# Three chunks instead of two open the later stages of a four-stage float32 block, and VectorE turns two groups of x

## The chip, the cores and the metric

The kernel runs on one core of a Trainium2 chip. The metric is device time in microseconds for one execution, the median of several runs. TensorE multiplies (PE in the profile, PEld its weight loads), VectorE is DVE, ScalarE is ACT, GpSimd is POOL, and the sync engine SP issues the DMAs. SBUF is the on-chip memory; the eight banks of PSUM take TensorE's results.

## What is computed

256 tokens of width 2048 go through two layers of a first block and one layer of a second, all float32. Cut to what matters here:

```python
def first_block(x, ...):
    for layer in range(2):
        h = rms_norm(x, mix_pre_g[layer])
        m = pool_conformer_mixer(h, ...) if layer == 0 else short_conv_mixer(h, ...)
        x = x + rms_norm(m, mix_post_g[layer])
        h = rms_norm(x, ffn_pre_g[layer])
        x = x + rms_norm(sq_relu_mlp(h, ffn_w1[layer], ffn_w2[layer]), ffn_post_g[layer])
    return x

def short_conv_mixer(h, w_in, conv_w, w_out):
    z = h @ w_in                       # b_gate, c_gate, u of 2048 each
    return (b_gate * causal_depthwise_conv(c_gate * u, conv_w)) @ w_out

def sq_relu_mlp(h, w1, w2):
    a = relu(h @ w1)                   # 2048 -> 8192
    return (a * a) @ w2                # 8192 -> 2048

def hybrid_layer(x, ...):              # the second block
    proj = rms_norm(x, norm_g) @ w_in  # q, k, v, z_a, u_b, v_b, z_b, g_a, g_b
    # q and k are normed per head; attention, a gated unit, two projections, and
    return x + merged @ w_out
```

## The kernel before

**Stages.** There are five: the first mixer, the first MLP, the short convolution, the second MLP, and the second block. `STAGE` holds their first chunks: 0, `C_M0`, `C_L1`, `C_M1`, `C_L2`. A chunk is 512 columns of a weight matrix (`chunk_table`), and its result fills two PSUM banks, one for each tile of 128 tokens.

**Steps.** A step is 256 rows of a chunk's weights. Each weight is split in two parts, w_hi (ScalarE, `split_hi`, L800) and w_lo (VectorE, `split_lo`, L818, which needs w_hi), and so is each activation, in buffers A and B. A step takes 12 matmuls of 128x512: two k-tiles, two token tiles, and lo x hi, hi x lo, hi x hi (L839 to L841). A chunk has 8 steps, or 4 where its depth is 1024. `SEQ` is the order of all steps, written by hand; `POS` gives a step's place in it. The text counts steps from the start of a stage. There are 6 slots for split weights and 3 for raw ones; a raw slot holds two steps.

**Order of work.** Every engine's program is a loop over the same steps. In its loop for step s, ScalarE or VectorE first splits the weights of step s + 3 and then does what the tables put at step s. Their queues are strictly in that order: what stands in the loop for step 34 comes after the split of step 37's weights. At a chunk's last step ScalarE waits until TensorE has done the chunk and evicts it (L1101). So the split of the fourth step after a chunk's last step stands behind the eviction, on ScalarE and, since w_lo needs w_hi, on VectorE.

**The opening of a stage.** x is updated in four groups of 512 columns, turned, scaled and split into A before the first matmul of a stage can use a group. Two chunks share the opening: their first four steps each, which need groups 0 and 1, then their last four, which need group 2 (first two of them) and group 3. TensorE turns groups 0 and 1 tile by tile (`turn_tile`, L907) and group 2 with `turn_x` (`turn`, L890) into the four small banks 4 to 7; VectorE turns group 3 in blocks of 32 by 256 (`turn_last`, L1525), four blocks at each of four steps. `hi_turned` and `lo_turned` cast it into A.

**Turning the hidden tiles.** In an MLP stage a pair of up chunks makes two tiles of 512 hidden features; four down chunks use them. ScalarE evicts a tile to z with a relu, GpSimd squares it, and VectorE turns it, 16 blocks in `TURN_STEPS` = 8 steps, two at each (`turn_hidden`, `turn_blocks`, L1944). `TURN_AT` gives the first step. After the last, ScalarE casts the high part (L1456) and VectorE the low part (L1984). In an MLP stage the order is chunks 0 and 1 (up, first pair), 2 and 3 (up, second pair), 4 to 7 (down, first pair). Chunk 3 takes steps 24 to 31 and chunk 4 steps 32 to 35. A down chunk's first two steps need the pair's first tile, its last two the second tile.

**Short convolution and last stage.** Chunks 0 to 2 of the short convolution make c, u and b of the first 512 features; VectorE multiplies c and u, turns the product and b, convolves (`short_conv`), and gates. In the last stage chunks 0 to 3 make q and k: ScalarE evicts and squares, VectorE sums per head (L2047) at the step after the chunk's end, scales (L2060) two steps later, and turns from the step that `QK_TURNS` gives, as (steps after the chunk's end, steps to spread over).

**Banks.** Chunk c uses main banks 2 (c % 2) and the next, and may start when chunk c - 2 has been evicted.

## Time and profile before

| | us |
|---|---|
| median of 3 runs | 2673.4 |
| lowest, highest | 2673.11, 2673.76 |
| the profiled run | 2673.97 |
| span of the profiled execution | 2672.2 |
| TensorE busy | 2665.8 |
| VectorE busy | 1960.7 |
| ScalarE busy | 1289.1 |
| GpSimd busy | 286.3 |

The span is the time from the first to the last instruction on the core; the run is a little longer. Busy times are those of one execution. A matmul's row gives a duration that overlaps the next matmul's, so TensorE's pace is read from the starts of its rows. The idle time in brackets at the end of a row is the engine's own, ahead of that row, with what ended it.

### The profile page before, as it was taken

All of it is one profiled execution on the core that took longest, in us unless ns stands there. A gap on an engine that the chain in (4) does not pass through costs nothing.

```text
span 2672.2 us, 31094 instructions
## 1 busy us (share of the span) xinstructions
PE 2665.8 (100%) x11905; PEld 2207.6 (83%) x11905; DVE 1960.7 (73%) x2706; ACT 1289.1 (48%) x1625; POOL 286.3 (11%) x263
## 2 busy tenths in 40 slices
PE   9999999999999999999999999999999999999999
PEld 7888888888888888888888888888888888888887
DVE  6888867666766787777777676668668869985574
ACT  6875544444444454444544444344455545544452
POOL 4841100000000010000100000000011001000000
PEclk9999999999999999999999999999999999999999
DMA  7555665555655556555556655555555655565554
GB/s 257 189 174 189 209 202 189 189 189 189 205 188 190 199 185 214 190 196 196 190 190 205 204 186 184 198 189 192 190 186 189 208 178 174 175 217 192 189 203 143
DMA packets 268148, 515.57 MB, mean 193 GB/s; under 512 B 8498, under 2 KB 28260, under 8 KB 267492
## 3 DMA queue, kind: packets, MB, share of 16 engines
q1 hardware_dynamic: 267732, 513.34, 57.3%
q8 instruction: 97, 1.59, 0.2%
q14 instruction: 47, 0.39, 0.0%
q10 hardware_dynamic: 272, 0.26, 0.0%
HBM read 511.47 MB, written 2.10 MB: 192 GB/s over the span
## 4 chain that ended last, share of the span: by engine, by line
PE 99%; DVE 0%; DMA 0%; ACT 0%; issue 0%; SPq 0%; DVEq 0%; ACTq 0%
PE bank L839 32%; PE bank L841 32%; PE bank L840 32%; PE bank L890 0%; PE bank L907 0%; PE bank L1062 0%; DMA x_res<-in_x 0%; DMA w_raw<-in_ab_w_in 0%; DVE w_lo L818 0%; PE bank L1076 0%; DVE tap_product L2083 0%; DVE z L2071 0%; PE bank L1048 0%; PE bank L1086 0%; PE bank L1085 0%; PE bank L1027 0%
## 5 line engine op out<-in xcount | busy, mean ns | idle before, releaser
L818 DVE TENSOR_TENSOR w_lo<-w_raw,w_hi 128x1024 fp32r<-128x1024 f32 x950 | 1182.4, 1263 | 439.5 <-ACT w_hi L800 433.0
L800 ACT ACTIVATE w_hi<-w_raw 128x1024 fp32r<-128x1024 f32 x954 | 973.0, 1056 | 615.6 <-PE bank L841 417.9
L839 PE MATMUL bank<-w_hi,A_lo 128*128 128x512 f32 x2432 | 950.6, 391 | 0.9 <-DVE w_lo L808 0.8
L841 PE MATMUL bank<-w_hi,A_hi 128*128 128x512 f32 x2432 | 946.8, 389 | 0.0
L840 PE MATMUL bank<-w_lo,A_hi 128*128 128x512 f32 x2432 | 946.5, 389 | 0.0
L839 PE MATMUL bank<-w_hi,B_lo 128*128 128x512 f32 x1408 | 548.6, 390 | 0.0
L841 PE MATMUL bank<-w_hi,B_hi 128*128 128x512 f32 x1408 | 547.8, 389 | 0.0
L840 PE MATMUL bank<-w_lo,B_hi 128*128 128x512 f32 x1408 | 547.8, 389 | 0.0
L839 PEld LDWEIGHTS bank<-w_hi,A_lo 128*128 128x128 f32 x2432 | 456.6, 188 | 97.7 <-DVE w_lo L808 2.2
L841 PEld LDWEIGHTS bank<-w_hi,A_hi 128*128 128x128 f32 x2432 | 456.5, 188 | 95.2
L840 PEld LDWEIGHTS bank<-w_lo,A_hi 128*128 128x128 f32 x2432 | 456.7, 188 | 93.5
L841 PEld LDWEIGHTS bank<-w_hi,B_hi 128*128 128x128 f32 x1408 | 264.3, 188 | 54.9
L839 PEld LDWEIGHTS bank<-w_hi,B_lo 128*128 128x128 f32 x1408 | 264.3, 188 | 54.7
L840 PEld LDWEIGHTS bank<-w_lo,B_hi 128*128 128x128 f32 x1408 | 264.3, 188 | 54.6
L1944 DVE STREAM_TRANSPOSE conv_out<-z 32x256 f32<-32x256 f32 x512 | 223.2, 436 | 10.5
L1101 ACT ACTIVATE z<-bank,small 128x512 f32<-128x512 f32 x108 | 68.5, 686 | 328.0 <-PE bank L841 320.8
L2247 POOL TENSOR_TENSOR z<-z 128x512 f32<-128x512 f32 x64 | 65.3, 1041 | 1094.1 <-ACT z L1101 1094.1
L1971 DVE TENSOR_TENSOR acc<-bank,acc 128x512 f32<-128x512 f32 x96 | 61.8, 686 | 85.7 <-PE bank L841 85.7
L2128 POOL TENSOR_TENSOR acc<-acc,gain_row 128x512 f32<-128x512 f32 x32 | 41.0, 1298 | 518.3 <-ACT bank L1172 477.7
L1456 ACT ACTIVATE B_hi<-conv_out 128x512 fp32r<-128x512 f32 x64 | 37.1, 628 | 99.6 <-DVE conv_out L1944 99.6
L2122 POOL TENSOR_TENSOR small<-small,neg_half 128x1 f32<-128x1 f32 (+2 forms) x21 | 34.3, 1633 | 298.9 <-DVE small L1498 280.7
L1944 DVE STREAM_TRANSPOSE conv_in<-z 32x256 f32<-32x256 f32 x128 | 55.8, 436 | 2.6
(176 smaller groups left out, 991.6 us busy)
## 6 DMA issues: line engine op xcount, KB each, us to landing
w_raw<-in_ffn_w SPq DMA_DIRECT2D x256, 1024.0 KB, 5.3
w_raw<-in_w_in SPq DMA_DIRECT2D x88, 1024.0 KB, 5.0
w_raw<-in_sc_w_in SPq DMA_DIRECT2D x48, 1024.0 KB, 5.1
w_raw<-in_ab_w_out SPq DMA_DIRECT2D x16, 1024.0 KB, 5.0
w_raw<-in_sc_w_out SPq DMA_DIRECT2D x16, 1024.0 KB, 5.0
w_raw<-in_w_out SPq DMA_DIRECT2D x16, 1024.0 KB, 5.0
w_raw<-in_ab_w_in SPq DMA_DIRECT2D x26, 512.0 KB, 4.9
w_raw<-in_ab_w_in SPq DMA_DIRECT2D x8, 1024.0 KB, 5.1
```

The source lines that it names most:

```text
L800: e.activation(w_hi[:, s % SPLIT_SLOTS, :], raw_step(s), ACT.Copy).then_inc(hi_made, 1)
L818: e.tensor_tensor(w_lo[:, slot, :], raw_step(s), w_hi[:, slot, :].bitcast(F32), ALU.subtract).then_inc(lo_made, 1)
L839: e.matmul(ps, lo[:, kt, tok], wh, start=first, stop=False)
L840: e.matmul(ps, hi[:, kt, tok], wl, start=False, stop=False)
L841: ins = e.matmul(ps, hi[:, kt, tok], wh, start=False, stop=last)
L1101: e.activation(out(tt), main_bank(c, tt), func, scale=rs(layer_of(c))[:, tt:tt + 1]).then_inc(act_took(c, tt), 1)
L1456: e.activation(halves["B"][0][:, kt:kt + 2, :], h_T[:, 2 * h:2 * h + 2, :], ACT.Copy).then_inc(hi_cast("h", layer, b, j, h), 1)
L1944: ins = e.transpose(dst[feat, :, :].rearrange("p k (t c) -> p t k c", t=NT)[:, :, :, tok], src[tok, :, :].rearrange("p t (k c) -> p t k c" ...
L1971: e.tensor_tensor(out, main_bank(c, tt), out, ALU.add).then_inc(dve_took(c, tt), 1)
L2122: e.tensor_tensor(out, cols(n, "mean", *key), neg_half[:, 0:n], ALU.pow).then_inc(root_made(*key), 1)
L2128: e.tensor_tensor(out, out, gain_row[:, c], ALU.mult).then_inc(gained(p, n, tt), 1)
L2247: e.tensor_tensor(z[:, s, tt, :], z[:, s, tt, :], z[:, s, tt, :], ALU.mult).then_inc(squared(layer, b, j, tt), 1)
```

## The change

The opening of stages 1 to 4 takes three chunks: the first four steps of chunks 0, 1 and 2, then the last four of chunks 0 and 1 in turns of two steps, then the last four of chunk 2. Chunk 0 ends with step 17 (it was 11), chunk 1 with step 19 (15), chunk 2 with step 23 as before. Chunk 2 uses the small banks 4 and 5, and starts when the last cast from them is done. TensorE turns groups 0 and 1 of x only. VectorE turns group 2 at steps 3 to 7 and group 3 at steps 8 to 12 (`X_TURNS`), and the casts stand at steps 9 and 14 (`X_HALVES`).

What hangs on the ends of chunks 0 and 1 moves: the hidden tiles of an MLP's first pair are turned in 7 steps each, at steps 19 to 25 and 27 to 33 (they were turned at 13 to 20 and 22 to 29), and cast at steps 26 and 34 (21 and 30). In the short convolution the product is turned at steps 20 to 27 (16 to 23) and b at 28 to 35 (24 to 31). In the last stage the four tiles of q and k are turned at steps 21 to 25, 26 to 30, 31 to 35 and 36 to 40 (15 to 20, 21 to 26, 27 to 31 and 35 to 39).

```diff
 TURN_STEPS = 8
+BY_VECTOR = (2, 3)
+X_TURNS = {2: (3, 5), 3: (8, 5)}
+X_HALVES = {2: 9, 3: 14}
 STEP_K = 2
...
-QK_TURNS = [(3, 6), (5, 6), (3, 5), (3, 5)]
+QK_TURNS = [(3, 5), (6, 5), (7, 5), (4, 5)]
...
-                for half in range(2):
-                    SEQ += [(c, 4 * half + i) for c in (first, first + 1) for i in range(4)]
-                rest = first + 2
+                SEQ += [(first + n, i) for n in range(3) for i in range(4)]
+                for half in range(2, 4):
+                    SEQ += [(c, 2 * half + i) for c in (first, first + 1) for i in range(2)]
+                SEQ += [(first + 2, i) for i in range(4, 8)]
+                rest = first + 3
...
+        def hidden_steps(b):
+            return 7 if b == 0 else TURN_STEPS
+
         TURN_AT = {}
         for layer in range(2):
             free = 0
             for b in range(NB):
                 for j in range(2):
                     TURN_AT[layer, b, j] = max(free, S_END[up_chunk(layer, b, j)] + 1)
-                    free = TURN_AT[layer, b, j] + TURN_STEPS + 1
+                    free = TURN_AT[layer, b, j] + hidden_steps(b) + 1
...
-        x_T = conv_out_flat[:, GK * TOK:2 * GK * TOK].rearrange("p (k t) -> p k t", k=GK)
+        x_T = {2: conv_out_flat[:, GK * TOK:2 * GK * TOK].rearrange("p (k t) -> p k t", k=GK),
+               3: conv_out_flat[:, 0:GK * TOK].rearrange("p (k t) -> p k t", k=GK)}
...
+        THIRD = [STAGE[p] + 2 for p in range(1, 5)]
+
         def main_bank(c, tt):
-            return bank[2 * (c % 2) + tt]
+            return bank[4 + tt if c in THIRD else 2 * (c % 2) + tt]
...
-            if i == 0 and c >= 2:
-                for tt in which:
-                    sem, value = taken(c - 2, tt)
-                    e.wait_ge(sem, value)
+            if i == 0 and c in THIRD:
+                e.wait_ge(lo_cast.sem, lo_cast.of("pre", THIRD.index(c) + 1, 1, 1, 1))
+            elif i == 0 and c >= 2:
+                for before in (c - 4, c - 2) if c - 2 in THIRD else (c - 2,):
+                    for tt in which:
+                        sem, value = taken(before, tt)
+                        e.wait_ge(sem, value)
...
-                if (c, i) == (C_L1 + 1, 0):
-                    turn_x(2, 2)
...
-                if (c, i) == (STAGE[p] + 1, 0):
-                    hi_x(p, 2)
-                if (c, i) == (STAGE[p] + 1, 1):
+                n = POS[c, i] - S0[STAGE[p]]
+                if n == 5:
                     statistics(p)
-                if (c, i) == (STAGE[p], 4):
-                    hi_turned(p)
+                for g in BY_VECTOR:
+                    if n == X_HALVES[g]:
+                        hi_turned(p, g)
...
-            def turn_last(p, n):
-
-                if n == 0:
-                    e.wait_ge(x_made.sem, x_made.of(p - 1, NG - 1, 1))
-                tok = slice(32 * n, 32 * n + 32)
-                for q in range(4):
-                    feat = slice(32 * q, 32 * q + 32)
-                    ins = e.transpose(x_T[feat, :, :].rearrange("p k (t c) -> p t k c", t=NT)[:, :, :, tok],
-                                      x[tok, :, D - CH:].rearrange("p t (k c) -> p t k c", k=GK)[:, :, :, feat])
-                if n == 3:
-                    ins.then_inc(x_turned(p), 1)
-
-            def lo_turned(p):
+            def lo_turned(p, g):
...
-                n = POS[c, i] - S0[STAGE[p]] - 3
-                if 0 <= n < 4:
-                    turn_last(p, n)
-                if (c, i) == (STAGE[p] + 1, 3):
-                    lo_turned(p)
+                at_step = POS[c, i] - S0[STAGE[p]]
+                for g in BY_VECTOR:
+                    if at_step == X_HALVES[g]:
+                        lo_turned(p, g)
+                for g in BY_VECTOR:
+                    first, steps = X_TURNS[g]
+                    n = at_step - first
+                    if 0 <= n < steps:
+                        if n == 0:
+                            e.wait_ge(x_made.sem, x_made.of(p - 1, g, 1))
+                        ins = turn_blocks(e, x[:, :, g * CH:(g + 1) * CH], x_T[g], n, steps)
+                        if n == steps - 1:
+                            ins.then_inc(x_turned(p, g), 1)
...
-                if part == 2 and j < NG:
-                    if i == 0:
-                        e.wait_ge(dve_took.sem, dve_took.of(c - 1, 1))
-                        if j > 0:
-                            e.wait_ge(short_made.sem, short_made.of(j - 1, SHORT_K - 1, GK - 1))
-                    ins = turn_blocks(e, z[:, z_slot("c", j), :, :], short_in[:, :, SPAD:], i)
-                    if i == TURN_STEPS - 1:
-                        ins.then_inc(c_turned(j), 1)
+                for j in range(NG):
+                    made = C_L1 + 3 * j + 1
+                    n = POS[c, i] - S_END[made]
+                    if 0 <= n < TURN_STEPS:
+                        if n == 0:
+                            e.wait_ge(dve_took.sem, dve_took.of(made, 1))
+                            if j > 0:
+                                e.wait_ge(short_made.sem, short_made.of(j - 1, SHORT_K - 1, GK - 1))
+                        ins = turn_blocks(e, z[:, z_slot("c", j), :, :], short_in[:, :, SPAD:], n)
+                        if n == TURN_STEPS - 1:
+                            ins.then_inc(c_turned(j), 1)
                 for k in range(NG):
-                    n = POS[c, i] - S0[C_L1 + 3 * k + 3] - (1 if k == NG - 1 else 0)
+                    n = POS[c, i] - S0[C_L1 + 3 * k + 3] - (4 if k == 0 else 1 if k == NG - 1 else 0)
...
-            ins = turn_blocks(e, z[:, z_slot("h", layer, b, j), :, :], h_T, n)
-            if n == TURN_STEPS - 1:
+            ins = turn_blocks(e, z[:, z_slot("h", layer, b, j), :, :], h_T, n, hidden_steps(b))
+            if n == hidden_steps(b) - 1:
                 ins.then_inc(turned(layer, b, j), 1)
...
                 for b in range(NB):
                     for j in two:
                         n = POS[c, i] - TURN_AT[layer, b, j]
-                        if 0 <= n < TURN_STEPS:
+                        if 0 <= n < hidden_steps(b):
                             turn_hidden(e, layer, b, j, n)
-                        if n == TURN_STEPS:
+                        if n == hidden_steps(b):
...
```

The first place is VectorE's queue in an MLP stage, around the end of chunk 3 (z is the tile that is turned, B_lo the low part of the hidden tile). Before, from the split of step 34 on:

```order
L818 TENSOR_TENSOR w_lo<-w_raw,w_hi 128x1024 [waits hi_made]
L1944 STREAM_TRANSPOSE conv_out<-z 32x2x4x32 [waits lo_cast,squared]
L1944 STREAM_TRANSPOSE conv_out<-z 32x2x4x32
L818 TENSOR_TENSOR w_lo<-w_raw,w_hi 128x1024 [waits hi_made]
L1944 STREAM_TRANSPOSE conv_out<-z 32x2x4x32 x2
```

Now, from the split of step 35 to what follows the split of step 37:

```order
L829 TENSOR_TENSOR w_lo<-w_raw,w_hi 128x1024 [waits hi_made]
L1944 STREAM_TRANSPOSE conv_out<-z 32x2x4x32 x2
L829 TENSOR_TENSOR w_lo<-w_raw,w_hi 128x1024 [waits hi_made]
L1944 STREAM_TRANSPOSE conv_out<-z 32x2x4x32 x3
L829 TENSOR_TENSOR w_lo<-w_raw,w_hi 128x1024 [waits hi_made]
L1984 TENSOR_TENSOR B_lo<-conv_out,B_hi 128x512 [waits hi_cast] x2
```

Before, the second hidden tile had been cast four steps earlier and the first tile of the next pair was being turned here; now the last pieces of the second tile, with one of three blocks, and its cast stand behind the splits of steps 35 to 37.

The second place is ScalarE's queue at the same steps, from the eviction of chunk 3 (bank2, bank3) on. Before:

```order
L1101 ACTIVATE z<-bank2,small 128x512 [waits step_done,turned,root_made]
L1101 ACTIVATE z<-bank3,small 128x512 [waits step_done]
L800 ACTIVATE w_hi<-w_raw 128x1024 [waits step_done]
L800 ACTIVATE w_hi<-w_raw 128x1024 [waits step_done,raw_loaded1]
L800 ACTIVATE w_hi<-w_raw 128x1024 [waits step_done]
L800 ACTIVATE w_hi<-w_raw 128x1024 [waits step_done,raw_loaded2]
L1179 ACTIVATE acc<-bank0 128x512 [waits step_done]
```

Now:

```order
L1104 ACTIVATE z<-bank2,small 128x512 [waits step_done,turned,root_made]
L1104 ACTIVATE z<-bank3,small 128x512 [waits step_done]
L811 ACTIVATE w_hi<-w_raw 128x1024 [waits step_done]
L811 ACTIVATE w_hi<-w_raw 128x1024 [waits step_done,raw_loaded1]
L811 ACTIVATE w_hi<-w_raw 128x1024 [waits step_done]
L1459 ACTIVATE B_hi<-conv_out 128x512 [waits turned]
L1459 ACTIVATE B_hi<-conv_out 128x512
```

The high part of the second hidden tile has moved behind the eviction and the three splits after it.

The third place is VectorE's queue in the last stage, behind the split of step 23 (acc<-z are the blocks of q and k, the reductions are the sums per head, z<-z the scaling). Now:

```order
L2060 TENSOR_TENSOR z<-z,small 128x512 [waits root_made]
L2060 TENSOR_TENSOR z<-z,small 128x512
L2047 TENSOR_REDUCE small<-conv_in 128x8 [waits square_made]
L1501 TENSOR_SCALAR small<-small 128x8 [waits total_made]
L829 TENSOR_TENSOR w_lo<-w_raw,w_hi 128x1024 [waits hi_made]
L1944 STREAM_TRANSPOSE acc<-z 32x2x4x32 [waits normed]
L1944 STREAM_TRANSPOSE acc<-z 32x2x4x32 x2
L829 TENSOR_TENSOR w_lo<-w_raw,w_hi 128x1024 [waits hi_made]
L2060 TENSOR_TENSOR z<-z,small 128x512 [waits root_made]
```

Before, that work of the first chunk stood from step 12 on:

```order
L2047 TENSOR_REDUCE small<-conv_in 128x8 [waits square_made]
L1498 TENSOR_SCALAR small<-small 128x8 [waits total_made]
L818 TENSOR_TENSOR w_lo<-w_raw,w_hi 128x1024 [waits hi_made] x2
L2060 TENSOR_TENSOR z<-z,small 128x512 [waits root_made]
L2060 TENSOR_TENSOR z<-z,small 128x512
L818 TENSOR_TENSOR w_lo<-w_raw,w_hi 128x1024 [waits hi_made]
L1944 STREAM_TRANSPOSE acc<-z 32x2x4x32 [waits normed]
```

The scaling of the first tile and the sums of the second now stand between the same two splits, and the first blocks are turned at step 21 instead of 15.

## Rows read from the trace of the kernel before

**Rows 1.** The page: busy time and count, granted clock in 40 slices, chain.

```profile
PE 2665.8 (100%) x11905; PEld 2207.6 (83%) x11905; DVE 1960.7 (73%) x2706; ACT 1289.1 (48%) x1625; POOL 286.3 (11%) x263
...
PEclk9999999999999999999999999999999999999999
...
PE 99%; DVE 0%; DMA 0%; ACT 0%; issue 0%; SPq 0%; DVEq 0%; ACTq 0%
```

**Rows 2.** TensorE's waits: line, waited for: us in total, times, longest.

```profile
PE bank L942 <- POOL neg_half L2147: 1.6, 1, 1.6
```

**Rows 3.** Timeline of TensorE, first MLP: start, duration, engine, line, operation, count.

```profile
261.69 0.39 PE L841 MATMUL bank<-w_hi,A_hi 128*128 128x512 f32 x1
261.92 1.03 PE L890 MATMUL bank<-ident,x_res 128*128 128x128 f32 x8
...
266.01 0.39 PE L841 MATMUL bank<-w_hi,A_hi 128*128 128x512 f32 x1
...
271.00 0.39 PE L839 MATMUL bank<-w_hi,A_lo 128*128 128x512 f32 x1
...
303.63 0.39 PE L839 MATMUL bank<-w_hi,A_lo 128*128 128x512 f32 x1
```

**Rows 4.** Timeline of VectorE in the opening of the first MLP.

```profile
260.24 1.78 DVE L1525 STREAM_TRANSPOSE conv_out<-x_res 32x256 f32<-32x256 f32 x4
...
275.08 1.66 DVE L1537 SCALAR_TENSOR_TENSOR A_lo<-conv_out,par,A_hi 128x256 fp32r<-128x256 f32 x4
```

**Rows 5.** Timeline of the last stage from its step 16 on.

```profile
2043.37 0.39 PE L839 MATMUL bank<-w_hi,A_lo 128*128 128x512 f32 x1
...
2047.06 1.22 DVE L818 TENSOR_TENSOR w_lo<-w_raw,w_hi 128x1024 fp32r<-128x1024 f32 x1 [2.44 <-ACT w_hi L800]
...
2048.20 1.21 DVE L2047 TENSOR_REDUCE small<-conv_in 128x8 f32<-128x1024 f32 x1
...
2049.64 1.33 DVE L1944 STREAM_TRANSPOSE acc<-z 32x256 f32<-32x256 f32 x3
...
2050.99 1.23 DVE L818 TENSOR_TENSOR w_lo<-w_raw,w_hi 128x1024 fp32r<-128x1024 f32 x1
...
2052.25 1.34 DVE L1944 STREAM_TRANSPOSE acc<-z 32x256 f32<-32x256 f32 x3
...
2054.74 1.28 DVE L2060 TENSOR_TENSOR z<-z,small 128x512 f32<-128x512 f32 x2
...
2056.06 0.88 DVE L1944 STREAM_TRANSPOSE acc<-z 32x256 f32<-32x256 f32 x2
```

**Rows 6.** Timeline of the first MLP, from step 32 (336.27) to 34 (341.71).

```profile
336.27 0.39 PE L839 MATMUL bank<-w_hi,B_lo 128*128 128x512 f32 x1
...
336.56 1.27 ACT L1101 ACTIVATE z<-bank,small 128x512 f32<-128x512 f32 x2 [4.03 <-PE bank L841]
...
338.80 1.64 DVE L818 TENSOR_TENSOR w_lo<-w_raw,w_hi 128x1024 fp32r<-128x1024 f32 x1 [4.03 <-ACT w_hi L800]
...
341.71 0.39 PE L839 MATMUL bank<-w_hi,B_lo 128*128 128x512 f32 x1
...
342.63 0.88 DVE L1944 STREAM_TRANSPOSE conv_out<-z 32x256 f32<-32x256 f32 x2
...
344.78 0.89 DVE L1944 STREAM_TRANSPOSE conv_out<-z 32x256 f32<-32x256 f32 x2
```

**Rows 7.** Timeline: the two parts of a hidden tile, first MLP.

```profile
330.43 1.16 ACT L1456 ACTIVATE B_hi<-conv_out 128x512 fp32r<-128x512 f32 x2 [3.77 <-DVE conv_out L1944]
...
331.57 1.29 DVE L1984 TENSOR_TENSOR B_lo<-conv_out,B_hi 128x512 fp32r<-128x512 f32 x2
```

**Rows 8.** Timeline of the short convolution: VectorE's split of step 39, TensorE's step 39.

```profile
1050.04 4.63 DVE L818 TENSOR_TENSOR w_lo<-w_raw,w_hi 128x1024 fp32r<-128x1024 f32 x4 [0.25 <-ACT w_hi L800]
...
1054.85 0.39 PE L839 MATMUL bank<-w_hi,A_lo 128*128 128x512 f32 x1
```

**Rows 9.** Timeline of TensorE at the kernel's start.

```profile
1.59 2.82 PE L942 MATMUL bank<-ident 128*128 128x128 f32 x12 [1.59 <-POOL neg_half L2147]
```

More of the change, by code:

```diff
@@ L241, in small_banks @@
     for key in turn_order():
-        if key[0] == "pre" and key[1] > 0 and key[2] == NG - 1:
+        if key[0] == "pre" and key[1] > 0 and key[2] in BY_VECTOR:
             continue
@@ L472, in build @@
                                    ([(g, tt) for tt in tiles for g in gs] if 0 in gs else [(g, tt) for g in gs for tt in tiles])])
-        x_turned = signal("x_turned", [(p,) for p in range(1, 5)])
+        x_turned = signal("x_turned", [(p, g) for p in range(1, 5) for g in BY_VECTOR])
         tap_done = signal("tap_done", DVE_TAPS)
@@ L893, in turn_x @@
             def turn_x(p, g):
-                if p == 0:
-                    e.wait_ge(x_loaded[g], 16)
-                else:
-                    e.wait_ge(x_made.sem, x_made.of(p - 1, g, 1))
+                e.wait_ge(x_loaded[g], 16)
                 turn(lambda tt, f: x[:, tt, g * CH + f.start:g * CH + f.stop], "pre", p, g)
@@ L1000, in pe_program @@
             boundary(1)
-            pe_mlp(e, turn_x, 0)
+            for c, i in matmul_steps(e, 1):
+                pass
             boundary(2)
@@ L1006, in pe_program @@
                 j, part = divmod(c - C_L1, 3)
-                if (c, i) == (C_L1 + 1, 0):
-                    turn_x(2, 2)
             boundary(3)
-            pe_mlp(e, turn_x, 1)
+            for c, i in matmul_steps(e, 3):
+                pass
             boundary(4)
@@ L1016, in pe_program @@
                 r = c - C_L2
-                if (r, i) == (1, 0):
-                    turn_x(4, 2)
                 if (r, i) in ((11, 1), (13, 1)):
@@ L1064, in mix_pooled @@
                 ins.then_inc(aux_filled("mix", j, h), 1)
-        def pe_mlp(e, turn_x, layer):
-            p = 1 + 2 * layer
-            for c, i in matmul_steps(e, p):
-                if (c, i) == (up_chunk(layer, 0, 1), 0):
-                    turn_x(p, 2)
         def pe_attention(e, aux_begin, task, h):
@@ L1121, in hi_x, with hi_turned @@
                     hi_half(p, g, h)
-            def hi_turned(p):
-                e.wait_ge(x_turned.sem, x_turned.of(p))
+            def hi_turned(p, g):
+                e.wait_ge(x_turned.sem, x_turned.of(p, g))
                 for h in two:
                     for k in (2 * h, 2 * h + 1):
-                        kt = GK * (NG - 1) + k
-                        ins = e.activation(halves["A"][0][:, kt, :], x_T[:, k, :], ACT.Copy, scale=par_col(PRE_COL[p], kt))
-                    ins.then_inc(hi_cast("pre", p, NG - 1, h), 1)
+                        kt = GK * g + k
+                        ins = e.activation(halves["A"][0][:, kt, :], x_T[g][:, k, :], ACT.Copy, scale=par_col(PRE_COL[p], kt))
+                    ins.then_inc(hi_cast("pre", p, g, h), 1)
             def hi_tile(p, g, tt):
@@ L1451, in act_mlp @@
                     for j in two:
-                        if POS[c, i] == TURN_AT[layer, b, j] + TURN_STEPS:
+                        if POS[c, i] == TURN_AT[layer, b, j] + hidden_steps(b):
                             e.wait_ge(turned.sem, turned.of(layer, b, j))
@@ L1516, in lo_x @@
                     lo_half(p, g, h)
-            def turn_last(p, n):
-                if n == 0:
-                    e.wait_ge(x_made.sem, x_made.of(p - 1, NG - 1, 1))
-                tok = slice(32 * n, 32 * n + 32)
-                for q in range(4):
-                    feat = slice(32 * q, 32 * q + 32)
-                    ins = e.transpose(x_T[feat, :, :].rearrange("p k (t c) -> p t k c", t=NT)[:, :, :, tok],
-                                      x[tok, :, D - CH:].rearrange("p t (k c) -> p t k c", k=GK)[:, :, :, feat])
-                if n == 3:
-                    ins.then_inc(x_turned(p), 1)
-            def lo_turned(p):
+            def lo_turned(p, g):
                 hi, lo = halves["A"]
                 for h in two:
-                    e.wait_ge(hi_cast.sem, hi_cast.of("pre", p, NG - 1, h))
+                    e.wait_ge(hi_cast.sem, hi_cast.of("pre", p, g, h))
                     for k in (2 * h, 2 * h + 1):
-                        kt = GK * (NG - 1) + k
-                        ins = e.scalar_tensor_tensor(lo[:, kt, :], x_T[:, k, :], par_col(PRE_COL[p], kt),
+                        kt = GK * g + k
+                        ins = e.scalar_tensor_tensor(lo[:, kt, :], x_T[g][:, k, :], par_col(PRE_COL[p], kt),
                                                      hi[:, kt, :].bitcast(F32), ALU.mult, ALU.subtract)
-                    ins.then_inc(lo_cast("pre", p, NG - 1, h), 1)
+                    ins.then_inc(lo_cast("pre", p, g, h), 1)
             def lo_part(p, g, tt, h):
@@ L1642, in early @@
             def early(p, c, i):
-                if (c, i) == (STAGE[p] + 1, 0):
-                    lo_x(p, 2)
-                n = POS[c, i] - S0[STAGE[p]] - 3
-                if 0 <= n < 4:
-                    turn_last(p, n)
-                if (c, i) == (STAGE[p] + 1, 3):
-                    lo_turned(p)
+                at_step = POS[c, i] - S0[STAGE[p]]
[11 more added lines that the diff above has]
+                            ins.then_inc(x_turned(p, g), 1)
                 if (c, i) == (STAGE[p], 4):
```

## The prediction

> **What bounds the kernel now.** I read the shares of the engines first, then the chain that ended last, then the list of who waited for whom. TensorE is busy for 2665.8 of 2672.2 us and makes up 99% of the chain, its granted clock is full in all 40 slices, and its longest wait, 1.6 us, lies at the start [rows 1, 2]. VectorE is at 73% and ScalarE at 48%. So the time is TensorE's instruction stream, and an edit has two ways to act: take instructions out of that stream, or make TensorE wait where it now waits for nothing. The average of 73% for VectorE says nothing of the second; that has to be read at each deadline.
>
> TensorE's pace: a step is 12 matmuls. Step 8 of the first MLP stage starts at 271.00 and step 20 at 303.63 [rows 3], so a step takes 32.63 / 12 = 2.719 us and a matmul 0.2266 us.
>
> **What is removed.** In each of four stages TensorE no longer turns the third group of x (8 transposes). With them, 15 matmul starts lie between 261.69 and 266.01 [rows 3]: 4.32 us where 15 x 0.2266 = 3.40 are due. So the 8 transposes, with the slower matmuls right behind them, cost 0.92 us, and four stages save **3.7 us**. ScalarE's and VectorE's casts of that group stay, reading SBUF in place of a bank.
>
> **What is added on VectorE.** 16 blocks of 32 by 256 per stage, beside the 16 there were. Prices from rows: 4 blocks 1.79 [rows 4]; 3 blocks 1.35 and a weight split in front of a transpose 1.26 (2049.64 to 2050.99 to 2052.25), a split in front of anything else 1.14 (2047.06 to 2048.20), a reduction with its small mean 1.44 (2048.20 to 2049.64), a head scaling 1.32 (2054.74 to 2056.06) [rows 5]. All of it hides as long as no step's operands come late. Four deadlines get near.
>
> Deadline 1, the opening: the fourth group's first half is needed by step 16 (it was step 10, the third group's was step 8 and is now 12). VectorE starts turning at 260.24 [rows 4] in either kernel and never waits until then: 32 blocks in pieces of 3 and 4, 8 x 1.35 + 2 x 1.79 = 14.4; the splits of steps 6 to 17, eight of them ahead of a transpose, 12 x 1.14 + 8 x 0.12 = 14.6; the third group's low parts 1.66 [rows 4], two of the fourth's 0.8, the mean 0.1. Sum 31.6, so 291.8. Step 16 starts at 303.63 - 4 x 2.719 - 0.92 = 291.8. A tie: I take 0.1 us a stage, **0.4** in all, and 0 to 0.3 a stage as its bounds. The third group (about 279 against step 12 at 280.9) and the third chunk's banks, last used by casts that are long done, cost nothing; ScalarE is idle there, as it loses its wait for TensorE's transposes.
>
> Deadline 2, the MLP stages. The first two chunks now end after steps 17 and 19 instead of 11 and 15, because the third chunk's four steps lie between. So the first hidden tile is turned at steps 19 to 25 and the second at 27 to 33, and the second is cast in VectorE's step 34 (it was step 30). TensorE needs it for step 34, the third step of the first down chunk. The two numbers are the same, and the question is how far VectorE runs ahead there. It doesn't: chunk 3 ends with step 31, ScalarE has to evict it before it splits the weights of step 35, and VectorE's split stands behind that, idle 4.03 us, until 338.80 where TensorE started step 32 at 336.27 [rows 6]. From then on VectorE does split and turn, split and turn: its own step 33 turns at 342.63, its step 34 turns at 344.78, while TensorE reached step 34 at 341.71 [rows 6]. In the changed kernel the same queue holds one more block at 342.63 (a piece of 3: +0.45), a split not followed by a transpose (-0.12), then the first low half of the hidden tile, 1.29 / 2 = 0.65 [rows 7], and 0.1 for the signal: 344.78 + 0.45 - 0.12 + 0.65 + 0.1 = 345.86. ScalarE's cast in between (it can start at 344.0, and half of it is 1.16 / 2 = 0.6 us [rows 7]) ends before that split does. TensorE waits 345.86 - 341.71 = 4.15 us, and restarts 0.1 slow, as behind every break in its stream. Two MLP layers (the second has the same rows 1051 us later): **8.5 us**. Bounds: 3.7, if a signal is faster than I think and the block's price falls, to 4.6 a layer.
>
> Deadline 3, the last stage. Its first two chunks end two steps apart, and what VectorE does for them (reductions, scalings, 3 x 16 blocks of queries and keys) is packed behind them with no gap. ScalarE's eviction and squares hold its queue as before: the split that follows starts 2047.06 - 2043.37 = 3.69 us behind the step after the chunk [rows 5]. After step 19 that is the split of step 23. From it to the split of step 39 the queue holds 17 splits, ten ahead of a transpose (20.6), 12 pieces of 3 and 3 of 4 (21.6), three reductions (4.3) and four scalings (5.3), 51.8 us in all. TensorE wants step 39 after 19 x 2.719 = 51.7 from the same mark. It gets it at 3.69 + 51.8 + 0.1 = 55.6: **3.9 us** late, taken in several small waits from step 29 on. Bounds 2.5 to 4.8, since a wait of ScalarE for VectorE's turn can come on top, and 1% of 56 us is 0.6.
>
> Deadline 4, the short convolution. Four pieces of two blocks of the b tile (0.89 each and 0.12 on the split before) now stand ahead of the split of step 39: that split starts at 1050.04 and would end at 1051.2, plus 4.0, plus 0.1 makes 1055.3 against step 39 at 1054.85 [rows 8]. **0.5 us**, bounds 0 to 1.2.
>
> **Sum.** 8.5 + 3.9 + 0.5 + 0.4 - 3.7 = +9.6 us. The profiled span of 2672.2 becomes 2681.8; its run took 2673.97, which is 0.6 above the median of 2673.4, and the median becomes **2683.0**.
>
> **Rivals.** (a) The clock. A wait of 4 us is longer than any in the rows now, and nothing in the middle of this trace shows what TensorE does after one. At the start, after 1.59 us without work, 12 transposes take 2.82 us, some 0.22 apart, where 8 later ones take 1.03, some 0.11 apart [rows 3, 9]: half speed, a loss of 12 x 0.11 = 1.3 us, although the granted clock is written as 1.00. If each MLP wait ends in such a stretch, 2 x 1.3 = 2.6 come on top: 2685.6. For it: the wait is long. Against it: at the start the engine had done nothing at all before. The Trainium skill (TensorE: Matmul & The Clock Gate, Part 1) says that the clock falls to 1.2 GHz after an idle stretch and comes back only with sustained work, and warns of idle gaps between matmuls; by its rule this rival holds, and the trace agrees as far as the start goes.
> (b) Not slower: the MLP wait does not come. That needs VectorE's queue ahead of the chunk's end by 4.2 us, so that the last pieces are turned before the eviction. Its place is step 31 to 34, and it decides from the point where the hidden tile's low half lands before 341.71. It would give 2683.0 - 8.5 = 2674.5, within 0.2% of before. The idle 4.03 us ahead of the split [rows 6] speaks against it: the queue isn't late by its own work but is held by its order. With the last stage hidden as well, only the removed transposes are left: about 2669.7.
> (c) The last stage's chain is hidden, since TensorE's need for step 39 comes later than the count says or VectorE's chain starts earlier: 2683.0 - 3.9 = 2679.1.
>
> **Numbers.** Forecast (2681 to 2685) 0.50; (a) 0.25; (c) 0.10; (b) with its further case 0.15. The range must leave out no more than 2 in 10: 2678.5 takes in (c) and leaves (b) out, 2687.5 takes in (a) with the upper bounds of deadlines 3 and 4. A measurement of this kernel tells about 0.2% (5.3 us) from no change: above 2678.7 are forecast, (a) and (c), 0.84; within it 0.14; faster by that much would need more than the 3.7 us that are there to be saved, 0.02.
>
> **What would show it.** Right: 32 fewer transposes by TensorE; in each MLP stage one TensorE wait of about 4 us for VectorE's low part of the hidden tile, at the first down chunk's third step; in the last stage several waits of about 1 us each for weight splits between its steps 29 and 39, VectorE without idle time before them; in the short convolution one of half a microsecond. Wrong: no wait of TensorE above 1 us between 300 and 345 us; or waits at step 16 of every stage of over 0.5 us, which would mean that I priced the blocks of x too low; or matmuls twice as far apart for some microseconds after the long waits, which is rival (a).

## The result and the profile after

| | before | after |
|---|---|---|
| median, us | 2673.61 (5 runs, 2673.11 to 2674.27) | 2689.44 (5 runs, 2687.14 to 2690.28) |
| ratio, 95% interval | | 1.0057 [1.0046, 1.0069] |
| the profiled run | 2673.97 | 2689.46 |
| its span | 2672.2 | 2687.7 |

The changed kernel is slower by 15.8 us, 6.4 more than forecast. From the page of the changed kernel, busy times with counts, the granted clock in 40 slices, and the chain that ended last:

```profile
PE 2669.7 (99%) x11873; PEld 2206.1 (82%) x11873; DVE 1988.7 (74%) x2770; ACT 1288.7 (48%) x1625; POOL 276.8 (10%) x263
...
PEclk9999999999999999999999999999999999999999
...
PE 95%; DVE 4%; ACT 0%; DMA 0%; issue 0%; SPq 0%; DVEq 0%; ACTq 0%
```

The counts answer to [rows 1]: 32 matmuls fewer on TensorE, 64 instructions more on VectorE. VectorE's average rose by one point only, and yet it now makes up 4% of the chain, where it had 0. TensorE's waits, in the form of [rows 2]. Its one line of 1.6 us still stands. These two are new:

```profile
PE bank L850 <- DVE B_lo L1984: 8.2, 2, 4.1
PE bank L850 <- DVE w_lo L829: 2.8, 5, 0.7
```

Two waits of 4.1 us are for the low part of a hidden tile, one in each MLP. Five waits of at most 0.7 us are for split weights, four of them in the last stage and one in the short convolution. These lines hold 11.0 us of new waits. They are not the whole difference, since the span is 15.5 us longer although 3.7 us of transposes went. The first mixer is the same program in both kernels, and it has waits that [rows 2] doesn't show: 0.8 us for a split and 0.5 for x before, 0.8 and 1.1 now.

**Where it lies.** The first transposes of x by TensorE at each stage's start mark the program off into five stretches. The timeline of TensorE, before, then after (start, duration, engine, line, operation, count):

```profile
244.60 0.60 PE L907 MATMUL bank<-ident,x_res 128*128 128x128 f32 x4
...
944.20 0.49 PE L907 MATMUL bank<-ident,x_res 128*128 128x128 f32 x3
...
1295.58 0.49 PE L907 MATMUL bank<-ident,x_res 128*128 128x128 f32 x3
...
1995.17 0.60 PE L907 MATMUL bank<-ident,x_res 128*128 128x128 f32 x4
```

```profile
245.30 0.49 PE L918 MATMUL bank<-ident,x_res 128*128 128x128 f32 x3
...
950.13 0.49 PE L918 MATMUL bank<-ident,x_res 128*128 128x128 f32 x3
...
1301.63 0.49 PE L918 MATMUL bank<-ident,x_res 128*128 128x128 f32 x3
...
2007.31 0.49 PE L918 MATMUL bank<-ident,x_res 128*128 128x128 f32 x3
```

| stretch, us | before | after | difference | by the prediction |
|---|---|---|---|---|
| first mixer | 244.60 | 245.30 | +0.70 | 0 |
| first MLP | 699.60 | 704.83 | +5.23 | +3.43 |
| short convolution | 351.38 | 351.50 | +0.12 | -0.32 |
| second MLP | 699.59 | 705.68 | +6.09 | +3.43 |
| last stage | 677.03 | 680.39 | +3.36 | +3.08 |
| sum | 2672.2 | 2687.7 | +15.5 | +9.6 |

The last column deals the terms of the sum out to the stretches: 4.25 for a wait with its restart, 0.1 for an opening, less 0.92 for the transposes. Of the 5.9 us that are missing, 1.80 and 2.66 lie in the MLPs, 0.7 in the two others, and 0.7 in the first mixer, which the change doesn't touch (there the wait for x from the DMA was 1.12 us in this execution and 0.54 in the one before).

**What is in the MLPs besides the wait.** TensorE's timeline of the changed kernel, from the last matmul before the wait (the brackets: idle time, and what ended it):

```profile
341.44 0.39 PE L852 MATMUL bank<-w_hi,B_hi 128*128 128x512 f32 x1
345.93 0.68 PE L850 MATMUL bank<-w_hi,B_lo 128*128 128x512 f32 x1 [4.10 <-DVE B_lo L1984]
346.41 0.63 PE L851 MATMUL bank<-w_lo,B_hi 128*128 128x512 f32 x1
346.83 0.63 PE L852 MATMUL bank<-w_hi,B_hi 128*128 128x512 f32 x1
...
348.97 0.61 PE L851 MATMUL bank<-w_lo,B_hi 128*128 128x512 f32 x1
349.39 0.41 PE L852 MATMUL bank<-w_hi,B_hi 128*128 128x512 f32 x1
```

The start of the next matmul comes 4.49 us after 341.44 in place of 0.23: a loss of 4.26. (The brackets say 4.10, since the row ahead is drawn 0.39 us long and the pace is 0.23. A wait costs 0.16 more than its brackets say, and then the restart.) Then, up to 349.39, matmuls start 0.43 us apart in place of 0.23. That is half speed for 3.5 us, and it loses another 1.68 (restart included: the first matmul behind a break takes some 0.1 us more than its pace, at full speed too). In the second MLP it is 12 matmuls and 2.58 us. The 40 slices of the page are too coarse to show it. Stretches of 10 us show it (length, busy us and count of PE, PEld, DVE, ACT, POOL, then the granted clock, DMA share, GB/s):

```profile
340.00:350.00 10.00, 5.90 (x20) 4.41 (x19) 8.15 (x13) 2.72 (x4) 0.00 (x0) 0.83 0.64 211
...
1400.00:1410.00 10.00, 7.76 (x23) 6.23 (x24) 4.58 (x7) 2.10 (x3) 0.00 (x0) 0.66 0.43 149
```

Full is 2.4 GHz and half is 1.2. A mean of 0.83 over 10 us is 3.4 us at half, which is the stretch of 0.43 us starts. A mean of 0.66 is 6.8 us at half. The slow starts behind the restart at 1402.24 fill only 5.3 of them, so the other 1.5 us lay in the wait. Matmuls twice as far apart behind the long waits are the sign that the prediction named for its rival (a).

### The profile page after: what moved, and what is told of

It is laid out like the page before. It is cut to its first block, busy times and chain, and to the rows that moved or that the text cites. A ratio compares the mean times of both kernels' runs of the same rounds, so it can differ in the third digit from the quotient of the medians.

```text
span 2687.7 us, 31090 instructions
## 1 busy us (share of the span) xinstructions
PE 2669.7 (99%) x11873; PEld 2206.1 (82%) x11873; DVE 1988.7 (74%) x2770; ACT 1288.7 (48%) x1625; POOL 276.8 (10%) x263
## 4 chain that ended last, share of the span: by engine, by line
PE 95%; DVE 4%; ACT 0%; DMA 0%; issue 0%; SPq 0%; DVEq 0%; ACTq 0%
PE bank L850 31%; PE bank L852 31%; PE bank L851 31%; DVE w_lo L829 2%; DVE acc L1944 1%; PE bank L918 0%; PE bank L1071 0%; DMA x_res<-in_x 0%; PE bank L904 0%; ACT w_hi L811 0%; DVE z L2060 0%; DVE conv_out L1944 0%; DMA w_raw<-in_ab_w_in 0%; ACT z L1104 0%; PE bank L1079 0%
## 5 line engine op out<-in xcount | busy, mean ns | idle before, releaser
L2122 POOL TENSOR_TENSOR small<-small,neg_half 128x1 f32<-128x1 f32 (+2 forms) x21 | 25.2, 1201 | 333.0 <-DVE small L1501 314.7
```

What stands on the lines that cost most here:

```text
L2122: e.tensor_tensor(out, cols(n, "mean", *key), neg_half[:, 0:n], ALU.pow).then_inc(root_made(*key), 1)
```

## Experiments

The first four ran on one chip beside the kernel before (2673.78 there), the next four on another (2673.91). For each the difference of every stretch to the kernel before, cut as above:

| kernel | median, us | first mixer | first MLP | short conv. | second MLP | last stage |
|---|---|---|---|---|---|---|
| changed kernel | 2689.44 | +0.70 | +5.23 | +0.12 | +6.09 | +3.36 |
| five steps | 2676.17 | +1.25 | -0.71 | +0.15 | -0.74 | +3.35 |
| short wait | 2682.09 | +0.16 | +3.19 | +0.13 | +1.50 | +3.42 |
| long wait | 2697.47 | -0.06 | +9.32 | +0.05 | +9.89 | +3.40 |
| q, k spread | 2684.62 | +0.20 | +6.28 | +0.08 | +5.01 | -0.87 |
| third chunk only | 2691.59 | -0.20 | +5.96 | +0.81 | +5.98 | +4.05 |
| all mended | 2670.21 | +0.19 | -0.93 | -0.88 | -0.95 | -1.03 |
| wait between | 2685.19 | -0.35 | +3.89 | +0.50 | +3.88 | +3.28 |
| busy wait | 2684.74 | +0.05 | +3.62 | +0.14 | +3.61 | +3.38 |

The first mixer is the same program in all of them, and its stretch spreads over 1.6 us. So the total of one profiled execution can't settle terms below some 1.5 us, and the stretches can.

### The MLP waits taken away

```diff
         def hidden_steps(b):
-            return 7 if b == 0 else TURN_STEPS
+            return 5 if b == 0 else TURN_STEPS
```

> The first pair's hidden tiles are turned in 5 steps each instead of 7 (hidden_steps 5), so the second is cast at VectorE's step 30, as before the change. Theory (order, then clock): both TensorE waits of 4.1 us vanish, 8.5 us with their restarts, and with them the stretches behind them in which matmuls stand 0.43 instead of 0.23 us apart (1.7 and 2.6 us in the trace of after): 2689.4 - 12.8 = 2676.6. Rival (the loss is the third chunk's own, through its banks or VectorE's blocks of x, and the clock falls by itself): only the waits go, 2681 or more.

Measured: 2676.17 (2675.51 to 2677.24), ratio 1.0009 [0.9999, 1.0018]. With the tile turned sooner no wait for B_lo is left, and no slow matmul. Each MLP falls from +5.23 and +6.09 to -0.71 and -0.74, which is the 0.92 of the transposes less the 0.2 that the opening now loses. So the MLP's excess, half-speed matmuls included, hangs on this one deadline, and but for the opening the rest of the change is off TensorE's path there. The rival fell.

### A wait of half the length

```diff
-        def hidden_steps(b):
-            return 7 if b == 0 else TURN_STEPS
+        def hidden_steps(b, j):
+            return 7 - j if b == 0 else TURN_STEPS
```

> Only the second tile of the first pair is turned in 6 steps instead of 7, so it is cast at VectorE's step 33: one split and a piece less ahead of it. The wait should be about 1.9 us instead of 4.1. Theory (the clock falls only behind the long wait): 2689.4 - 2 x 2.2 - 4.3 = 2680.7, matmuls 0.23 us apart right behind the wait. Rival (any wait of this kind brings half speed): 2689.4 - 4.4 = 2685.0.

Measured: 2682.09 (2680.61 to 2683.54), between the two. Both waits measure 1.95 us, and only one of them was followed by a fall. TensorE's timeline around the first and the second, and the stretches of 10 us with their granted clock:

```profile
340.96 0.39 PE L852 MATMUL bank<-w_hi,B_hi 128*128 128x512 f32 x1
343.30 0.47 PE L850 MATMUL bank<-w_hi,B_lo 128*128 128x512 f32 x1 [1.95 <-DVE B_lo L1984]
343.61 0.40 PE L851 MATMUL bank<-w_lo,B_hi 128*128 128x512 f32 x1
...
344.80 0.63 PE L850 MATMUL bank<-w_hi,B_lo 128*128 128x512 f32 x1
...
1397.58 0.47 PE L850 MATMUL bank<-w_hi,B_lo 128*128 128x512 f32 x1 [1.95 <-DVE B_lo L1984]
```

```profile
340.00:350.00 10.00, 8.05 (x28) 6.15 (x28) 7.71 (x12) 3.05 (x4) 0.00 (x0) 0.83 0.61 210
...
1390.00:1400.00 10.00, 8.05 (x36) 6.37 (x35) 7.65 (x12) 6.21 (x8) 2.04 (x2) 1.00 0.43 152
```

After the first wait five matmuls start at full speed, and the slow ones begin at 344.80, 1.5 us after the restart. They lose 1.68 us. After the second wait none is slow, and between 1397 and 1407 us the granted clock was 1.00. So the same wait at the same step of the two MLP stages cost 2.2 us in one and 3.8 in the other. The six runs agree: the fastest, 2680.61, has a mean granted clock of 1.000, the five others, 2681.73 to 2683.54, have 0.999. What decides between the two isn't shown.

### A wait of twice the length

Nine blocks that nobody reads are turned ahead of the second tile's last piece.

```diff
+            if (b, j, n) == (0, 1, hidden_steps(b) - 1):
+                for m in range(9):
+                    turn_blocks(e, z[:, z_slot("h", layer, b, j), :, :], x_T[2], m, 16)
             ins = turn_blocks(e, z[:, z_slot("h", layer, b, j), :, :], h_T, n, hidden_steps(b))
```

> Nine more blocks (into a place nobody reads) are turned ahead of the second tile's last piece, 9 x 0.45 = 4.0 us: the wait grows from 4.1 to 8.1 us in each MLP stage. Theory (half speed is a stretch of some fixed size behind a long wait): 2689.4 + 8.0 = 2697.4, the slow stretches 1.6 to 3 us of loss each as now. Rival (the loss of the clock grows with the wait): 4 us more, 2701.5.

Measured: 2697.47 (2696.49 to 2698.43), ratio 1.0089 [1.0074, 1.0104]. The waits are 8.03 us. What the slow matmuls add is 1.82 and 2.41 us, 4.23 in all, against 1.68 and 2.58, 4.26 in all, in the changed kernel. So the clock's price comes once for each fall and didn't grow with the wait, and the rival fell. The first restart and the granted clock there:

```profile
349.11 0.77 PE L850 MATMUL bank<-w_hi,B_lo 128*128 128x512 f32 x1 [8.03 <-DVE B_lo L1987]
```

```profile
340.00:350.00 10.00, 1.98 (x7) 1.39 (x6) 9.79 (x19) 2.10 (x3) 0.00 (x0) 0.80 0.37 109
```

A clock of 0.80 in these 10 us means 4 us at half, but only the last 0.9 of them lie behind the restart at 349.11. Some 3 us of the half level were spent while TensorE stood still: the clock had fallen before the work came back.

### The last stage's chain

```diff
-QK_TURNS = [(3, 5), (6, 5), (7, 5), (4, 5)]
+QK_TURNS = [(3, 8), (9, 7), (12, 7), (11, 5)]
```

> Only QK_TURNS changes: the four tiles of q and k are turned at steps 21 to 28, 29 to 35, 36 to 42 and 43 to 47, so nine blocks fewer stand ahead of the split of step 39 (4.0 us). Theory (VectorE's queue is the bound from step 23 to 39 of the last stage): the waits for weight splits there, 3.3 us with 0.6 of restarts in the trace, vanish, 2689.4 - 3.8 = 2685.6. Rival (the waits come from ScalarE, which waits for VectorE's turns before it splits): under 1.5 us is won.

Measured: 2684.62 (2684.36 to 2685.74), 4.8 below the changed kernel. The last stage falls from +3.36 to -0.87, by 4.2 us, and 0.5 lies in the first mixer. Of five waits for split weights one is left, the short convolution's:

```profile
PE bank L850 <- DVE w_lo L829: 0.5, 1, 0.5
```

The same number of blocks is turned here. Only their density behind the ends of the first two chunks differs, and so it was the cause.

### The third chunk alone

VectorE turns only the fourth group, as before, and TensorE turns the third group into the small banks. The rest is the changed kernel.

```diff
-BY_VECTOR = (2, 3)
-X_TURNS = {2: (3, 5), 3: (8, 5)}
-X_HALVES = {2: 9, 3: 14}
+BY_VECTOR = (3,)
+X_TURNS = {3: (8, 5)}
+X_HALVES = {3: 14}
...
-                pass
+                if (c, i) == (C_M0 + 1, 0):
+                    turn_x(1, 2)
```

> Three chunks open each later stage and everything else is timed as in the changed kernel, but TensorE turns the third group of x again (8 transposes a stage, 32 in all) and VectorE turns only the fourth. It tests the price of the removed transposes and of VectorE's extra blocks. Theory: +3.7 us for 4 x 0.92 of TensorE, -0.8 us for the waits at the opening's step 16, which go when VectorE has 16 blocks less to turn: 2689.4 + 2.9 = 2692.3. The waits in the MLP and the last stage stay (4.1 us twice, three of about 0.8 us), since they hang on the later ends of the first two chunks and not on the blocks of x. Rival: VectorE's 16 more blocks a stage are what makes it late in the MLP and in the last stage too; then those waits shrink and the time falls below 2687.

Measured: 2691.59 (2690.58 to 2692.65), ratio 1.0066 [1.0052, 1.0079]. The short convolution and the last stage each come out 0.69 above the changed kernel, which is 0.92 for the transposes less 0.2 for the opening. The waits stay:

```profile
PE bank L850 <- DVE B_lo L1996: 8.2, 2, 4.1
PE bank L850 <- DVE w_lo L829: 2.7, 5, 0.7
```

So VectorE's 16 further blocks a stage are paid for: they bring 0.69 us a stage. The waits in the MLPs and the last stage come from the order, from the later ends of the first two chunks.

### All waits moved away

The edits of the first and the fourth experiment, and

```diff
-X_HALVES = {2: 9, 3: 14}
+X_HALVES = {2: 9, 3: 13}
...
-                    n = POS[c, i] - S0[C_L1 + 3 * k + 3] - (4 if k == 0 else 1 if k == NG - 1 else 0)
+                    n = POS[c, i] - S0[C_L1 + 3 * k + 3] - (2 if k == 0 else 1 if k == NG - 1 else 0)
```

> The changed kernel with every wait it brought in moved away: the hidden tiles of an MLP's first pair turned in 5 steps each in place of 7, the four query and key tiles turned at (3, 8), (9, 7), (12, 7), (11, 5) in place of (3, 5), (6, 5), (7, 5), (4, 5), the fourth group of x cast at step 13 in place of 14, and the short convolution's b tile turned two steps later. Theory: from the run with 5 steps (2676.2) another 4.8 us go with the last stage's waits, as between the changed kernel and the run with the tiles spread, and up to 0.7 in the short convolution and 0.8 in the openings: 2670 to 2671.4, below the kernel before (2673.6) by the 3.7 us of the transposes. Rival: the mended places compete for the same time of VectorE, and what goes at one deadline comes back at another: 2674 or more.

Measured: 2670.21 (2669.45 to 2671.78), ratio to the kernel before 0.9986 [0.9978, 0.9995], faster by 3.7 us. All of TensorE's waits and the marks of its stretches:

```profile
PE bank L953 <- POOL neg_half L2147: 1.6, 1, 1.6
PE bank L904 <- DMA x_res<-in_x: 0.6, 1, 0.6
```

```profile
244.79 0.38 PE L918 MATMUL bank<-ident,x_res 128*128 128x128 f32 x2
...
943.46 0.60 PE L918 MATMUL bank<-ident,x_res 128*128 128x128 f32 x4
...
1293.96 0.49 PE L918 MATMUL bank<-ident,x_res 128*128 128x128 f32 x3
...
1992.60 0.49 PE L918 MATMUL bank<-ident,x_res 128*128 128x128 f32 x3
```

The four stretches come out at -0.93, -0.88, -0.95 and -1.03, and 0.92 was worked out for the transposes from [rows 3]. This is the gain that the changed kernel spent on its waits.

### A wait between the two

The short wait's kernel, with two more blocks turned:

```diff
+            if (b, j, n) == (0, 1, hidden_steps(b, j) - 1):
+                for m in range(2):
+                    turn_blocks(e, z[:, z_slot("h", layer, b, j), :, :], x_T[2], m, 16)
```

> As the run with 7 and 6 steps for the hidden tiles, with two more blocks turned by VectorE (into a buffer that nobody reads there) ahead of the second tile's last ones: TensorE's wait in each MLP is some 0.9 us longer, 2.8 in place of 1.95. It tests how long a wait has to be before the clock falls behind it. At 1.95 us it fell behind one wait of the two that were profiled, at 4.1 and 8.0 us behind all six. If the clock falls behind a wait of 2.8 us each time: 2682.1 + 2 x 0.9 + 2.4 for the second fall = 2686.3. If it falls behind one in two, as at 1.95: 2683.9. If not at all: 2681.9.

Measured: 2685.19 (2683.88 to 2686.49), the middle of the first two expectations. The waits are 2.73 us, and in the profiled execution the clock fell behind both, at 1.68 us each. With that size in place of the 2.4 that the expectation took, a fall each time makes 2682.1 + 1.6 + 1.7 = 2685.4. The four runs spread over 2.6 us, so how often it falls is not settled by them.

### The wait filled with work

```diff
+            def busy_turns(n):
+                hi = halves["A"][0]
+                for _ in range(n):
+                    e.matmul(bank[6], hi[:, 0, 0:P], hi[:, 0:2, :], start=True, stop=True)
...
             for c, i in matmul_steps(e, 1):
-                pass
+                if (c, i) == (C_M0 + 4, 1):
+                    busy_turns(18)
```

The same stands in the second MLP.

> The changed kernel, but in each MLP stage TensorE does 18 matmuls of 128x512 that nobody uses, into a small bank that is free, between the first down chunk's second and third steps, that is while it would wait for VectorE's low part of the hidden tile: 18 x 0.2266 = 4.08 us in place of 4.1 us without work. It tests whether the half-speed stretch behind the wait comes from the idleness itself. Theory: the low part comes as late as before, but no matmul behind it is slow: 2689.4 - 4.2 = 2685.2, and the matmuls behind the gap lie 0.22 us apart from the first. Rival: the slow stretch comes from the operands (the weights' or the hidden tile's supply), and stays: 2689.4.

Measured: 2684.74 (2684.60 to 2684.78), 4.7 below the changed kernel. TensorE's timeline, and stretches with their granted clock:

```profile
341.04 4.24 PE L954 MATMUL bank<-A_hi 128*128 128x512 f32 x18
345.30 0.47 PE L850 MATMUL bank<-w_hi,B_lo 128*128 128x512 f32 x1
345.61 0.40 PE L851 MATMUL bank<-w_lo,B_hi 128*128 128x512 f32 x1
345.84 0.39 PE L852 MATMUL bank<-w_hi,B_hi 128*128 128x512 f32 x1
```

```profile
340.00:350.00 10.00, 9.98 (x45) 7.97 (x44) 7.55 (x12) 2.11 (x3) 0.00 (x0) 1.00 0.62 210
...
1400.00:1410.00 10.00, 9.99 (x44) 8.31 (x45) 4.52 (x8) 4.41 (x7) 0.00 (x0) 1.00 0.32 105
```

The operand comes as late as before: VectorE's cast of it starts 3.43 us after the step was due in both kernels. The useful work stands still for 4.26 us as before. But the matmuls behind it start 0.23 apart at once. The MLPs fall from +5.23 and +6.09 to +3.62 and +3.61. So idleness of TensorE is what costs the clock here, not the supply of operands, and its price was 1.61 and 2.48 us. The clock is at 1.000 in all four runs, which spread over 0.18 us, where the changed kernel's five spread over 3.1.

## Why the prediction was right and wrong

**What bounds the kernel, and the transposes removed: right.** 0.92 us for 8 transposes was forecast, and -0.88 to -1.03 a stage is left where nothing waits.

**Deadline 1, the opening: right that it is a tie, too low in size.** Step 16 starts 0.11 to 0.15 us late in all four stages (in the first MLP at 292.62), and its first matmul takes 0.08 more: 0.2 a stage, 0.8 in all against 0.4, within the bounds. The casts one step earlier take it away.

**Deadline 2, the MLP waits: right in their place, cause and size.** VectorE's timeline in the changed kernel, to be held against [rows 6]:

```profile
338.75 1.64 DVE L829 TENSOR_TENSOR w_lo<-w_raw,w_hi 128x1024 fp32r<-128x1024 f32 x1 [3.13 <-ACT w_hi L811]
...
342.58 1.34 DVE L1944 STREAM_TRANSPOSE conv_out<-z 32x256 f32<-32x256 f32 x3
343.96 1.23 DVE L829 TENSOR_TENSOR w_lo<-w_raw,w_hi 128x1024 fp32r<-128x1024 f32 x1
345.10 1.28 DVE L1984 TENSOR_TENSOR B_lo<-conv_out,B_hi 128x512 fp32r<-128x512 f32 x2
```

VectorE still stands idle ahead of the split that waits for the eviction, then turns three blocks where it turned two, splits, and casts. The wait was forecast as 4.15 us from the start that was due to the one that came, and it measured 4.26 (341.67 to 345.93). With the restarts the two MLPs lose 8.7 us where 8.5 were forecast. That the restart itself came at 345.93, where 345.86 was forecast, is in part luck: the removed transposes bring everything there 0.92 us forward, which the forecast left out, and the first mixer's 0.70 and the opening's 0.2 took it back.

**Deadline 3, the last stage: right.** 3.9 us were forecast with the waits from step 29 to step 39. TensorE's first one is at step 30, and its three longest were alike. These are the four of the last stage:

```profile
2093.88 0.50 PE L850 MATMUL bank<-w_hi,A_lo 128*128 128x512 f32 x1 [0.67 <-DVE w_lo L829]
...
2111.19 0.50 PE L850 MATMUL bank<-w_hi,A_lo 128*128 128x512 f32 x1 [0.68 <-DVE w_lo L829]
...
2117.61 0.50 PE L850 MATMUL bank<-w_hi,A_lo 128*128 128x512 f32 x1 [0.67 <-DVE w_lo L829]
...
2134.90 0.50 PE L850 MATMUL bank<-w_hi,A_lo 128*128 128x512 f32 x1 [0.31 <-DVE w_lo L829]
```

Excess of the starts over 0.2266, restarts included: 0.17 at step 29 (2090.19), 0.95, 0.95 and 0.93 at steps 30, 36 and 38 (the first three rows), 0.34 at step 39 (2120.70), 0.58 at step 44 (the last row). That is 3.9 us. The last lies behind step 39, where the chain was no longer followed, and up to step 39 it is 3.3, so a part of the agreement is luck. VectorE has no idle time from 2086 to 2134, as the prediction wanted.

**Deadline 4, the short convolution: right within its bounds**, 0.77 in place of 0.5.

**What failed is rival (a), in odds and in size.** The sum of the prediction let TensorE come back at full speed behind each MLP wait and held no term for the clock. As a rival it gave the fall a quarter of the chance and 2.6 us. It came each time, and cost 4.26 us in the profiled execution. With it the sum of the changed kernel closes: 0.7 in the first mixer, -3.7 for the transposes, 8.5 for the MLP waits, 4.3 for the slow starts with the restarts behind them, 3.9, 0.8 and 0.8 for the last stage, the short convolution and the openings make 15.3 of the 15.5 us. The case that it took for the likeliest was the one in which TensorE comes back at full speed, and its one argument against the fall, that "at the start the engine had done nothing at all before", was no argument from a row: behind all eight waits of 4 us and more that were profiled, which follow dense work, the clock was low too. The size was the second error. 12 x 0.11 prices twelve transposes. Even in the execution that the prediction had, the spacing of 0.11 begins only behind 4.68 us. That is some 3.1 us at half speed, or 1.5 a wait, and would have made rival (a) 2686.1. And that execution was a short case. The one of the kernel with five steps, which came later, shows the half speed going on at the same place in the same program:

```profile
1.58 2.82 PE L953 MATMUL bank<-ident 128*128 128x128 f32 x12 [1.58 <-POOL neg_half L2147]
...
4.55 1.11 PE L966 MATMUL bank<-ident,x_res 128*128 128x128 f32 x4
5.46 1.91 PE L953 MATMUL bank<-ident 128*128 128x128 f32 x8
```

There it lasts to 7.19, 5.6 us at half speed. The price of a fall is half of the stretch that lies behind the restart. Over the eight waits of 4 us and more that were profiled (the changed kernel, long wait, q and k spread, third chunk only) it was 1.47 to 2.67 us with a mean of 2.0. Two falls of at most half of 5.6 put rival (a) as high as 2683.0 + 5.6 = 2688.6, and with 2.0 each, restarts left out of the 8.5 so as not to count them twice, it is 2686.8. Both figures are hindsight. Of the 2.6 us left up to 2689.44, 0.7 lie in the short convolution and the last stage, 0.7 in the first mixer, 0.2 in the MLPs' openings, and some 0.5 in the MLP waits and falls, 12.8 in place of the 12.3 in this sum. The other 0.6 come from the kernel before, whose profiled run lay above its median where the changed kernel's did not.

The Trainium skill (TensorE: Matmul & The Clock Gate, Part 1) says the clock stands at 1.2 GHz by default after idleness, that the time at the low clock is a budget of time and not a number of matmuls, and that it differs from run to run. The traces here agree on all three. Behind a wait of 2.7 us or more the half-speed starts fill 3.0 to 5.6 us, and the granted clock there reads 1.2 GHz. Some 5.6 us held 24 transposes at the start of the kernel with five steps, and 13 matmuls of 128x512 behind the first long wait of the kernel with q and k spread. The same program had falls of different length. The prediction had used the page for the sign alone, and counted instructions.

**The range.** It ended at 2687.5, since it took rival (a) at 1.3 a wait with the upper bounds of deadlines 3 and 4. With 2.8 a wait, which no row of that time showed, it would have ended near 2690.5 and held the time. With the 1.5 that the start's rows gave, it would still have missed.

## What to carry to other kernels

A wait of TensorE of some microseconds is priced as the wait plus a fall of its clock. The fall costs about 2 us here. The means behind waits of 2.7, 4 and 8 us are 1.7, 2.0 and 2.1, which lie closer together than single falls behind the same wait of 4.1 us (1.47 to 2.67). Waits of 0.2 to 0.7 us (five in the changed kernel, over thirty in all that were profiled) cost only the delay of the start and 0.1 for each restart. So one long wait is worth filling with matmuls that nobody uses, even where its cause can't be removed: that gave back 1.61 and 2.48 us in the two MLPs here. Several short waits in place of a long one should do the same, which no run here tests.

When a reordering makes some result later, look for what the other engines queue behind it by step number: a buffer that is cast at step 34 and needed at step 34 is late by however far that engine's queue runs behind, and moving it ahead by four steps cost nothing here. A gain of 0.9 us a stage was used up by the first deadline that was missed, and showed in the time only with every deadline met.

## What the runs showed of the hardware

- Same wait, same step of the stage, different price: behind 1.95 us of idleness the clock fell in one of two profiled cases, behind 2.73 us in both, behind 4.1 and 8.0 us in all eight. Behind waits of up to 0.7 us it never fell, nor behind the one of 1.1 us in the changed kernel's first mixer.
- The fall can come late. Behind four waits some matmuls ran at full speed first: for 1.5 us behind one of 1.95, 0.8 behind one of 2.73, 0.8 and 1.3 behind the two of 4.1 in the kernel with the third chunk alone.
- The low level can begin during the wait: of 4 us at half between 340 and 350 us in the long wait's kernel, 3 lay ahead of the restart at 349.11, and 1.5 of 6.8 ahead of the changed kernel's second. Only the part behind the restart costs time.
- Falls are a part of the spread of a kernel's runs, and not all of it. The four runs with the filled waits, each with a granted clock of 1.000, spread over 0.18 us, and the changed kernel's five over 3.1. But the eleven runs with all waits moved away had 1.000 too and spread over 2.3 us. What moved those isn't shown.
- What stays open: how often the clock falls behind waits of 2 to 3 us, for which four profiled waits are too few.
